# Forget sums and causal mask by TensorE in the score banks, and the first scores ahead of the delta output's flip

## The reference

```
def forgetting_attention(q, k, v, log_f):
    c = jnp.cumsum(log_f.astype(f32), axis=1)
    ...
    s = jnp.einsum('bqhd,bkhd->bhqk', q_blk, kt) + cq_blk[..., None] - ck[:, :, None, :]
    s = jnp.where(key_pos[None, :] <= q_pos[:, None], s, -jnp.inf)
    p = jax.nn.softmax(s, axis=-1)
    return jnp.einsum('bhqk,bkhd->bqhd', p, vt)
```

## Time and profile before

| | us |
|---|---|
| median of 3 runs | 3163.26 |
| lowest and highest run | 3161.17, 3167.71 |
| the profiled execution, with what lies around its span | 3154.97 |
| its span | 3153.2 |
| TensorE busy | 2884.5 (91%) |
| VectorE busy | 1501.0 (48%) |
| ScalarE busy | 1137.2 (36%) |
| forgetting attention, layer 0 | 195.02 to 221.05 |
| output projection starts, layer 0 and 1 | 221.05, 722.12 |

### The profile page before, as it was taken

How to read it: one execution, slowest core, us unless ns; L and a number is a source line. 1 busy time by engine, 2 the same in 40 slices (tenths; PEclk the granted TensorE clock), 3 DMA queues, 4 the chain that set the end, 5 groups by cost and what they waited for, 6 DMA issues and landing times.

```text
span 3153.2 us, 67929 instructions
## 1 busy us (share of the span) xinstructions
PE 2884.5 (91%) x26308; PEld 1871.4 (59%) x26308; DVE 1501.0 (48%) x4806; ACT 1137.2 (36%) x3085; POOL 0.2 (0%) x4
## 2 busy tenths in 40 slices
PE   8979999978998989888988888989999999899998
PEld 7858887856555545555555554444444444557887
DVE  5641004564566666666666664783322200454321
ACT  3121002221566656565666652262211100243210
POOL 0000000000000000000000000000000000000000
PEclk9979999988999999999999998999999999999999
DMA  5444434364799999999999980101122211211441
GB/s 204 173 174 160 157 137 147 134 241 139 230 332 330 333 327 335 328 332 329 327 336 332 327 303 28 66 15 41 58 75 80 80 67 67 91 44 57 158 147 67
DMA packets 205858, 576.06 MB, mean 183 GB/s; under 512 B 6496, under 2 KB 6624, under 8 KB 179040
## 3 DMA queue, kind: packets, MB, share of 16 engines
q1 hardware_dynamic: 205536, 571.72, 52.5%
HBM read 570.65 MB, written 1.05 MB: 181 GB/s over the span
## 4 chain that ended last, share of the span: by engine, by line
PE 59%; DMA 21%; DVE 12%; issue 3%; ACT 3%; DVEq 1%; SPq 1%; ACTq 0%
PE P L497 44%; DMA ring<-ws_moe 20%; DVE arena L1894 4%; PE P L925 2%; DVE ring L1894 2%; PE P L686 1%; PE P L544 1%; PE P L608 1%; DVE small L1544 1%; PE P L618 1%; PE P L627 1%; DVEq L1891 1%; PE P L877 1%; PE P L576 1%; PE P L976 1%
## 5 line engine op out<-in xcount | busy, mean ns | idle before, releaser
L497 PE MATMUL P<-arena,ring 128*128 128x256 f32 (+1 forms) x2784 | 900.3, 484 | 24.7 <-ACT arena L1175 24.6
L497 PEld LDWEIGHTS P<-arena,ring 128*128 128x128 f32 x2784 | 531.9, 192 | 383.0 <-issue 335.4
L925 PE MATMUL P<-arena 128*32 128x256 f32 x6496 | 372.5, 381 | 6.0 <-DMA arena<-ws_moe 5.2
L925 PE MATMUL P<-ring,arena 128*32 128x256 f32 x4256 | 277.1, 409 | 75.6 <-DMA ring<-ws_moe 74.2
L497 PE MATMUL P<-X_sb,ring 128*128 128x256 f32 x1504 | 335.1, 384 | 2.2 <-ACT X_sb L1154 1.6
L497 PEld LDWEIGHTS P<-X_sb,ring 128*128 128x128 f32 x1504 | 287.5, 192 | 44.8 <-issue 3.1
L925 PEld LDWEIGHTS P<-arena 128*32 128x32 f32 x6496 | 215.0, 111 | 146.8 <-DMA arena<-ws_moe 9.7
L1894 DVE COPY arena<-ring 128x256 f32 x1008 | 211.6, 294 | 143.8 <-DMA ring<-ws_moe 138.8
L1377 ACT ACTIVATE arena<-ring 128x256 f32 x672 | 215.8, 406 | 170.0 <-DMA ring<-ws_moe 161.7
L925 PEld LDWEIGHTS P<-ring,arena 128*32 128x32 f32 x4256 | 148.7, 117 | 185.9 <-DMA ring<-ws_moe 86.7
L1894 DVE COPY arena<-arena 128x256 f32 x1008 | 211.8, 294 | 75.6 <-DMA arena<-ws_moe 58.4
(11 more groups left out here) (360 smaller groups left out, 2652.6 us busy)
## 6 DMA issues: line engine op xcount, KB each, us to landing
ring<-ws_moe SPq DMA_DIRECT2D x84, 2048.0 KB, 14.2
arena<-ws_moe SPq DMA_DIRECT2D x84, 2048.0 KB, 15.2
ring<-ws_b SPq DMA_DIRECT2D x137, 1024.0 KB, 4.8
ring<-ws_a SPq DMA_DIRECT2D x67, 1024.0 KB, 4.9
cst_sb<-cst SPq DMA_DIRECT2D x1, 1664.0 KB, 8.5
X_sb<-xT SPq DMA_DIRECT2D x1, 1024.0 KB, 4.9
X_sb<-ctxT SPq DMA_DIRECT2D x1, 1024.0 KB, 4.7
out<-Y SPq DMA_DIRECT2D x2, 512.0 KB, 2.6
```

Of the source, the lines that this page charges most:

```text
L497: ins = nc.tensor.matmul(bank(i, n), blockap(s, b % SLOT), rhs(kk), start=kk == 0, stop=kk == k - 1)
L925: ins = nc.tensor.matmul(acc(g // 2)[BR * j:BR * (j + 1), g % 2], x[:, b * BR:(b + 1) * BR], weights_of(b), start=k == 0, stop=last and kk ...
```

## The change

The three small matmuls and the copy `cc` are gone. The sums are copied from two partitions only, to `past_l`. During the delta rule ScalarE makes two-row operands of them: after its read in step 1 `past_r` = (c, 1), and after its read in step 2 `past_l` in place = (-1, c). In the attention each unit's score matmul stays open, and two more add to the same bank: the identity times the mask, into the last 128 keys, and `past_l` times `past_r`, a product over two rows, which is c at t minus c at s. VectorE's maximum and ScalarE's exponential then read the bank; `prep` and `SC` are gone. The scores of pair p go to banks (2p+i+2) mod 4 (`fox_bank`), and pair 0's are made before the wait for `delta_out` and the flip, which TensorE runs right behind them. Buffers `foxP` and `foxPT` move to other places in SBUF.

```diff
@@ -227,7 +227,8 @@
         MT = [YD, bd(8)]
-        CR = arena_at(19968, 1536).rearrange("p (h t) -> p h t", h=H1)
+        past_l = arena_at(19968, 1536)[0:2].rearrange("p (h t) -> p h t", h=H1)
+        past_r = arena_at(0, 1536)[0:2].rearrange("p (h t) -> p h t", h=H1)
         foxA = FM.rearrange("p k r t -> p (k r t)")[:, 0:1536]
@@ -265,7 +266,6 @@
-        cc = small[:, 336:348].rearrange("p (t c) -> p t c", t=TT)
@@ -286,9 +286,8 @@
         foxV = arena_at(11520, 768).rearrange("p (t c) -> p t c", t=TT)
-        SC = arena_at(0, 1024).rearrange("p (b c) -> p b c", b=4)
-        foxP = arena_at(1024, 1536).rearrange("p (b c) -> p b c", b=6)
-        foxPT = arena_at(2560, 1024).rearrange("p (b c) -> p b c", b=4)
+        foxP = arena_at(1536, 1536).rearrange("p (b c) -> p b c", b=6)
+        foxPT = arena_at(6912, 1024).rearrange("p (b c) -> p b c", b=4)
         PB = arena_at(16896, 3072).rearrange("p (b c) -> p b c", b=6)
@@ -339,6 +338,7 @@
         SQH = arena_at(0, 4096).rearrange("p (k c) -> p k c", k=KD)
+        second, less_first = cst[0:2, CST["ident"] + 1:CST["ident"] + 2], stat[0:2, 22:23]
         ln_eps, rms_eps = stat[:, 20:21], stat[:, 21:22]
@@ -397,6 +397,9 @@
                 eng.wait_ge(sem("summed"), NB * DOWN_AT[ph] + b + 1)
+
+        def fox_bank(u):
+            return P1[:, (u + 2) % 4]
 
@@ -595,7 +598,7 @@
 
-            def attention(pairs, qk, vfn, pb, ptb):
+            def attention(pairs, qk, vfn, pb, ptb, bias=None, between=None):
 
@@ -605,8 +608,11 @@
                         q, kk = qk(h + i, t, nk)
-                        nc.tensor.matmul(P1[:, (2 * p + i) % 4, 0:nk * P], q, kk, start=True, stop=True)\
-                            .then_inc(sem("scores"), 1)
+                        to = fox_bank(2 * p + i) if bias else P1[:, (2 * p + i) % 4]
+                        ins = nc.tensor.matmul(to[:, 0:nk * P], q, kk, start=True, stop=bias is None)
+                        if bias:
+                            ins = bias(to, h + i, t, nk)
+                        ins.then_inc(sem("scores"), 1)
 
@@ -631,6 +637,8 @@
                         scores(p)
+                    if p == 0 and between:
+                        between()
                     if p >= 3:
@@ -704,9 +712,6 @@
                 C.take("decay_read")
-                nc.tensor.matmul(P1[:, 3, 0:6], c_("tri"), lft[:, 0], start=True, stop=True)
-                nc.tensor.matmul(P1[:, 3, 6:12], c_("tri"), lft[:, 1], start=True, stop=False)
-                nc.tensor.matmul(P1[:, 3, 6:12], c_("ones"), lft[:, 0], start=False, stop=True)
                 for j in range(3):
@@ -826,17 +831,27 @@
                 ada_flip(P0[:, 2], 2, 0)
-                C.take("delta_out")
-                for r in range(6):
-                    ins = nc.tensor.transpose(P1[:, r // 3, r % 3 * P:(r % 3 + 1) * P],
-                                              O1[:, 2 * r:2 * r + 2, :].rearrange("p g d -> p (g d)"), c_("ident"))
-                ins.then_inc(sem("delta_flipped"), 1)
-                C.take("delta_read")
-                C.take("mod_ready", 6)
+
+                def forget(to, h, t, nk):
+
+                    nc.tensor.matmul(to[:, (nk - 1) * P:nk * P], c_("ident"), c_("neg"), start=False, stop=False)
+                    return nc.tensor.matmul(to[:, 0:nk * P], past_l[:, h, t * P:(t + 1) * P], past_r[:, h, 0:nk * P],
+                                            start=False, stop=True)
+
+                def delta_flip():
+
+                    C.take("delta_out")
+                    for r in range(6):
+                        ins = nc.tensor.transpose(P1[:, r // 3, r % 3 * P:(r % 3 + 1) * P],
+                                                  O1[:, 2 * r:2 * r + 2, :].rearrange("p g d -> p (g d)"), c_("ident"))
+                    ins.then_inc(sem("delta_flipped"), 1)
+                    C.take("delta_read")
+                    C.take("mod_ready", 6)
+
                 attention(FOX_PAIRS,
                           lambda h, t, nk: (foxq[h % 2 * HD:h % 2 * HD + HD, h // 2, t * P:(t + 1) * P],
                                             foxk[h % 2 * HD:h % 2 * HD + HD, h // 2, 0:nk * P]),
-                          lambda h, j: foxV[:, j, h * HD:(h + 1) * HD], foxP, foxPT)
+                          lambda h, j: foxV[:, j, h * HD:(h + 1) * HD], foxP, foxPT, forget, delta_flip)
                 linear_normed(f"out{l}", KD, lambda k: mix1[:, k, :], groups=(6, 7) if l else (6,))
@@ -1294,7 +1309,10 @@
                         ada_rows(8 * l + 4, 5 * l, 1, 2, 1)
+                    if n == 1:
+                        A.link(a.activation(past_r, past_l, ACT.Identity, scale=c_("ident", 1)[0:2], bias=second))
                     if n == 2:
+                        A.link(a.activation(past_l, past_l, ACT.Identity, scale=second, bias=less_first))
                         ada_rows(8 * l + 6, 5 * l + 1, 2, 2, 0)
@@ -1306,7 +1324,7 @@
                 warm(ACT.Exp)
-                attention(FOX_PAIRS, lambda u, w: SC[:, u % 4, 0:w], foxP, foxPT)
+                attention(FOX_PAIRS, lambda u, w: fox_bank(u)[:, 0:w], foxP, foxPT)
 
@@ -1564,6 +1582,7 @@
             L(v.memset(rms_eps, RMS_EPS))
+            L(v.tensor_scalar(less_first, c_("ident", 1)[0:2], -1.0, None, ALU.mult))
             for g, ng in neg_gain.items():
@@ -1645,8 +1664,7 @@
                 V.take("forget_sums")
-                L(v.tensor_copy(cc.rearrange("p t c -> p (t c)"), P1[:, 3, 0:12]))
-                L(v.tensor_copy(CR.rearrange("p h t -> p (h t)"), P1f[:, 0:1536]), "forget_read")
+                L(v.tensor_copy(past_l.rearrange("p h t -> p (h t)"), P1f[0:2, 0:1536]), "forget_read")
                 V.take("decay_exp")
@@ -1753,14 +1771,7 @@
 
-                def prep(u, h, t, w):
-
-                    dst = SC[:, u % 4, 0:w]
-                    L(v.scalar_tensor_tensor(dst, P1[:, u % 4, 0:w], cc[:, t, h:h + 1], CR[:, h, 0:w], ALU.add, ALU.subtract))
-                    L(v.tensor_tensor(SC[:, u % 4, w - P:w], SC[:, u % 4, w - P:w], c_("neg"), ALU.add))
-                    return dst
-
-                attention(FOX_PAIRS, prep, foxP,
+                attention(FOX_PAIRS, lambda u, h, t, w: fox_bank(u)[:, 0:w], foxP,
                           lambda hp, t, src: v.tensor_scalar(mix1[:, 5 + hp, t * P:(t + 1) * P], src, v_(f"mix{l}", 5 + hp),
```

## The result

| | before | after |
|---|---|---|
| median, us | 3165.49 (4 runs beside it) | 3190.48 |
| lowest and highest run | 3161.17, 3170.53 | 3188.89, 3191.20 |
| span of the profiled execution | 3153.2 | 3189.1 |
| gating to output projection, layer 0 | 192.79 to 221.05: 28.26 | 195.56 to 235.86: 40.30 |
| gating to output projection, layer 1 | 693.78 to 722.12: 28.34 | 707.36 to 747.67: 40.31 |

The ratio is 1.0075, with a 95% interval of 1.0063 to 1.0087. The forecast was 3143.4 us in a range of 3134 to 3153, and 0.86 for faster: wrong in size and in sign.

What follows compares the result with a forecast made beforehand. VectorE was taken to bound the forgetting attention, run twice. Savings of 16.4 us there, 2.3 at the projection's start and 1.2 at the sums made 19.9, from a median of 3163.26 to 3143.4 us, range 3134 to 3153.

Steps and rivals of the forecast that it cites:

- What bounds the kernel before: Forgetting attention at the end of each layer's delta stage: VectorE is the bound, busy 23.3 of 31 us in layer 0.
- Part 1: Attention: VectorE loses two of three operations ahead of each maximum, 9.3 us per layer; maxima from the bank cost nothing extra.
- Part 2: Attention: two more TensorE matmuls per unit, loads hidden; two pairs take 8.1 to 9.4 us at 1.2 GHz.
- Rival 4: Attention: four more exposed loads of 0.2 us per unit, 9.6 us per layer on TensorE; 3157.8 us, chance 4%.
- Part 3: Attention: the clock rises a few us into the stage and holds; projection 8.2 us early per layer, 16.4 for both.
- the forecast's own walk at 1.2 GHz without overlap: Attention: clock low throughout, sums' product not overlapping the score; projection at 223.2, 2.2 us late per layer.
- the forecast's warm 17.0: Attention at 2.4 GHz throughout: projection at 209.8, 11.2 us early per layer; as a rival 3135.1 us, chance 15%.
- Part 4: Attention's start: first scores made ahead of the flip remove VectorE's 0.95 us idle, counted in the 8.2 us per layer.
- Part 5: Output projection's start: first 32 matmuls lose 4.56 us over both layers to the low clock; half, 2.3, is regained.
- Part 6: Sums: three small matmuls and one VectorE copy go, 1.2 us for both layers; ScalarE's two added passes cost nothing.
- Rival 3: Attention: clock low, matmuls one behind the other, TensorE the bound at 9.4 us per two pairs; 3166.5 us, chance 4%.

Runs made afterwards that it cites:

- e9: The kernel before, VectorE's two operations ahead of each maximum cut to one addition of a prepared mask less keys' sums; 3148.35 us, ratio 0.9969 to before.
- e2: The changed kernel with a pair's matmuls ordered by kind (both scores, both masks, both two-row products); 3169.17 us, ratio 1.0034 to before.
- e5: The changed kernel with unused filler matmuls, three ahead of the wait for `delta_out` and two behind the flip; 3172.17 us, ratio 1.004 to before.
- e11: The changed kernel, same order, with the sums' product over 128 rows and unused filler matmuls, four ahead of the flip, two behind; 3141.29 us, ratio 0.9942 to before.
- e6: The changed kernel ordered by kind, product over 128 rows, unused filler matmuls, four ahead of the flip and two behind; 3133.47 us, ratio 0.9919 to before.
- e10: The changed kernel ordered by kind, two-row products kept, unused filler matmuls, four ahead of the flip and two behind; 3150.45 us, ratio 0.997 to before.
- e1: The kernel before with only the first pair's scores moved ahead of the delta flip; 3159.17 us, ratio 0.9998 to before.
- e3: The changed kernel, same order, with the sums' product over 128 rows (126 zero) instead of 2; 3168.32 us, ratio 1.0035 to before.
- e8: The changed kernel with one added matmul per unit (prepared mask less keys' sums), both scores first, plus unused filler matmuls; 3129.98 us, ratio 0.9905 to before.
- e4: The changed kernel ordered by kind and with the sums' product over 128 rows, no fillers; 3138.29 us, ratio 0.9935 to before.

## Why the prediction was wrong

**What bounds the kernel before** was right: e9 took 0.38 to 0.39 us off each unit, 4.6 per layer, and the stage gave 4.4 of it back.

**Part 1** was right: maxima out of PSUM take 0.29 and 0.42, and VectorE's busy time from the gating to the projection fell from 21.90 us to 13.45 in layer 0. That is 8.5 less; the forecast's 9.3 counted the gaps between operations too.

**Part 2 failed, at the load "behind the running matmul at no cost".** Per unit three loads are exposed, 0.30 us each at 1.2 GHz. That is 12 x 3 x 0.30 = 10.8 us per layer. A short pair was priced at 2.1 to 2.6 and took 4.33, a long one 3.4 to 4.3 and took 6.04. The row it rested on, 16 loads in 3.43 us beside 16 matmuls in 3.62, is of one shape repeated; the new order changes shape at every matmul. The trace of before does show such a change:

```profile
209.44 1.23 PE L608 MATMUL P<-MIX 64*128 64x256 f32 x4
210.59 0.69 PE L618 MATMUL P<-arena 128*64 128x128 f32 x4
```

Two heads' scores side by side stream in 0.85 us, and the next kind starts after 1.15. The same 0.30 stands in both durations of the earlier trace rows (1.23 is 0.85 + 0.30 and a tail of 0.08); the forecast took their difference, 1.23 - 0.80, and so it cancelled.

The Trainium skill has a rule (TensorE: Matmul & The Clock Gate, section on the mechanism of row and column tiling), by which a load overlaps a running matmul only where the row groups differ, or where it goes to a background weight buffer. Rival 4 priced the first half of it, 7.3 to 7.9 us for two pairs against VectorE's 3.8, which is a TensorE-bound stage. The runs agree with that half from score to mask and from mask to product. They disagree in the projection and between e2's two products, where the columns stream at full rate, and also from the even head's product (rows 0 and 1) to the odd head's score (rows 64 to 127), where the rows differ and 0.30 was paid all the same (209.74 to 210.89 in after). What no run can show is which loads go to that buffer. The forecast had set the rule aside on the strength of the one case.

**Part 3 failed, at "TensorE will run almost without a gap ..., so I take the clock to rise".** TensorE had almost no gap by its records (25.00 of 25 us busy from 200 to 225), and the clock read 0.50 for 40 us; from a warm start (e5) it even fell. The inference from the projection, where the earlier trace rows have 0.78 and the next stretch of that trace, 230 to 235, has 1.00, took busy time as the cause. The matmuls were of another kind there: full height, of one shape. With a product over 128 rows (e11, and e6 against e10) the clock holds.

How much of the miss is whose depends on which step is taken off first. The forecast had 212.8 - 192.79 = 20.0 us for the stage and got 40.3. With the clock up throughout and the order of after (e11, 128 rows) it takes 22.6; from there to 40.3 there are 17.7, which go with the low clock (a small part with the two rows: at 2.4 GHz 0.42 from mask to product in e5, 0.33 in e11). Taken the other way, the forecast's own walk at 1.2 GHz without overlap ends at 223.2, a stage of 30.4: the clock alone costs 10.4, and the exposed loads are the 9.9 on top, near the 10.8 above. So of the 20.3 us Part 2 carries 2.6 to 9.9 and Part 3 10.4 to 17.7. Of the 22.6 of e11, 3.4 go with the order (e6 has 19.2); the 2.2 that e6 lies above the forecast's warm 17.0 are not divided further.

**Part 4** was right (e1: 0.94 and 0.91 for 0.95).

**Part 5**: after gained nothing, its projection starting at 0.50 like that of before. Where the clock was up, the 32 records took 7.14 in both layers, 4.76 less than before in sum; the 4.56 was a sound size for a case that did not come.

**Part 6**: not settled. VectorE's copy of the sums takes 1.75 as before; the operation behind it starts at 45.05 instead of 45.36, and 0.3 us per layer is below what the start of the stage scatters by. ScalarE's two passes took 1.67 us each and lay in waits, as said:

```profile
172.88 1.67 ACT L1313 ACTIVATE arena<-arena,cst_sb 2x1536 f32<-2x1536 f32 x1
179.41 0.48 ACT L1309 ACTIVATE arena<-P 64x384 f32<-64x384 f32 x1 [4.86 <-PE P L812]
179.93 1.67 ACT L1315 ACTIVATE arena<-arena,small,cst_sb 2x1536 f32<-2x1536 f32 x1
```

**The rivals.** Rival 3 named the mechanism (cold, one behind the other, TensorE the bound from 8.5 us per two pairs on) and its last sentence the missing part, a load on top. With the 13.7 us that two pairs took in place of 9.4, its own sum would have been 3166.5 + 6 x 4.3, about 3192 (an estimate; 3190.48 was measured). It had a chance of 4%. Rival 4 had the loads, at 0.2 us about right for 2.4 GHz, but took the clock to be up. The case that came is both together: I had treated as alternatives two things that occur at once and make each other worse, 0.20 us of load becoming 0.30.

What stays open: why a load is exposed by 0.30, 0.15 or nothing (the row count of the neighbours goes with it, but so does which operand repeats), and by what the granted clock tells the two-row product from the wide one. For after's own order and cold start, more rows alone (e3) left the clock at 0.50 in the profile; there the order is needed too, and why is open.

## What to carry to other kernels

Additions moved from VectorE to TensorE are cheap only if they keep the stream of matmuls uniform: put matmuls of one kind together, use all 128 rows even where two carry data, and price each change of kind with a load (here 0.2 to 0.3 us). Price a TensorE stage from starts, not busy time, and don't take a full busy row as a promise that the clock rises. Where the addend can be prepared once, one matmul through the identity beats two, and one VectorE addition instead of two operations, with TensorE left alone, is already worth 8.8 us in the two stages, of the 21.7 that the best version takes off them (e9, e8). And subtract durations with care: what stands in both, here a load, goes out of the difference.

## What the hardware showed that was not expected

- Records 100% busy with the clock at 0.50 for 25 us and more (after, 200 to 225), and the same busy share with the clock rising in e4 (200 to 205). An exposed load leaves no gap between the matmul records, so busy time does not tell it from streaming.
- The clock fell while TensorE was 100% busy: in e5 1.00 over 198 to 199 us, 0.52 over 199 to 200, 0.50 behind, with 1.00 of 1 us busy in each from 196 on.
- A product over 2 of 128 rows, in the same place and with the same columns as one over 128, cost 0.14 to 0.16 us more per change at 1.2 GHz (0.72 against 0.58, 1.15 against 0.99), and from a warm start the clock fell with it (e5, and e10 in its profile and most executions) and held without it (e6, e11).
- Two kernels that differ only in those rows (e2 and e4) stand 31 us apart.
